# Second mixer's projection: each group's C tile moved to its sixth place, z tiles behind it

## The reference, cut to what matters

```python
proj = h @ in_w                                   # D_MODEL 1024 -> z 2048, xbc 3072, dt 64
z = proj[..., :SSD_D_INNER]
xbc = silu(_dwconv(proj[..., SSD_D_INNER:SSD_D_INNER + SSD_XBC], conv_w, conv_b))   # 5 taps
...
xh = xbc[..., :SSD_D_INNER]                       # 16 tiles of 128 columns, 4 a group
bm = xbc[..., SSD_D_INNER:SSD_D_INNER + gn]       # 4 tiles, 1 a group
cm = xbc[..., SSD_D_INNER + gn:]                  # 4 tiles, 1 a group
...
chunk_states = einsum('bcsgn,bcsgrp->bcgrpn', bm, xdt * decay_end[..., None])
def step(s, inp):
    st, dec = inp
    return s * dec[..., None, None] + st, s       # states at the chunks' starts
...
y = y * silu(z)
```

## Time and profile before

| what | before |
|---|---|
| median of 3 runs | 3686.03 us (3685.19 to 3686.39) |
| the profiled execution's own time | 3686.52 us |
| its span, first to last instruction | 3684.7 us |
| mean granted TensorE clock | 0.953 |
| TensorE busy | 3375.9 us (92%) |
| VectorE busy | 1864.7 us (51%) |
| ScalarE busy | 1276.8 us (35%) |

### The profile page before, as it was taken

The page is one execution under the profiler, slowest core; times in us unless marked ns, Lnnn a source line. Parts: engine busy times, 40 slices in busy tenths (PEclk is TensorE's granted clock), DMA queues, the critical chain, the costliest instruction groups (busy, mean ns, idle before and its releaser), DMA issues. The chain is left out here.

```text
span 3684.7 us, 58735 instructions
## 1 busy us (share of the span) xinstructions
PE 3375.9 (92%) x24055; PEld 2910.7 (79%) x24055; DVE 1864.7 (51%) x3039; ACT 1276.8 (35%) x2048; POOL 364.9 (10%) x356
## 2 busy tenths in 40 slices
PE   6999898977599999997899999789997499999998
PEld 4999674756599999996899999656664499999997
DVE  6333487765433333333545454599996533333334
ACT  4322323222133333223433233266664133332233
POOL 0000000000111111111010000000000011111111
PEclk8999898988799999998999999889998699999999
DMA  7666313254688888885243443498776488888887
GB/s 241 224 204 203 132 48 127 105 190 157 237 286 287 287 286 286 292 299 158 72 137 103 160 141 95 140 339 253 256 254 234 150 287 290 299 291 286 287 287 263
DMA packets 414015, 798.95 MB, mean 217 GB/s; under 512 B 21991, under 2 KB 108844, under 8 KB 412555
## 3 DMA queue, kind: packets, MB, share of 16 engines
q1 hardware_dynamic: 384940, 700.50, 54.1%
q0 software_dynamic: 28720, 96.31, 8.9%
q10 hardware_dynamic: 208, 0.10, 0.0%
HBM read 687.94 MB, written 108.90 MB: 216 GB/s over the span
## 5 line engine op out<-in xcount | busy, mean ns | idle before, releaser
L2441 PEld LDWEIGHTS moe_banks<-moe_xt,mix_ring 128*128 128x128 f32 x8192 | 1011.1, 191 | 5.7 <-issue 3.2
L2441 PE MATMUL moe_banks<-moe_xt,mix_ring 128*128 128x144 f32 x8192 | 1012.4, 287 | 3.1 <-ACT moe_xt L2485 3.1
L63 PE MATMUL ssd_banks<-h_leading,ssd_w_split 128*128 128x384 f32 x1920 | 416.8, 345 | 1.5 <-DVE ssd_w_split L3208 1.5
L2614 DVE TENSOR_TENSOR moe_hid<-moe_banks,moe_sg 128x128 f32<-128x128 f32 x256 | 74.7, 292 | 579.6 <-ACT moe_sg L2537 579.6
L2466 PE MATMUL moe_banks<-moe_down_parts,moe_hid_parts 128*128 128x512 f32 x1536 | 357.8, 392 | 0.0
L63 PEld LDWEIGHTS ssd_banks<-h_leading,ssd_w_split 128*128 128x128 f32 x1920 | 338.7, 189 | 16.1 <-issue 13.6
L2466 PEld LDWEIGHTS moe_banks<-moe_down_parts,moe_hid_parts 128*128 128x128 f32 x1536 | 285.8, 188 | 71.4 <-issue 13.2
L2557 DVE TENSOR_TENSOR moe_down_parts<-mix_ring,moe_down_parts 128x2048 fp32r<-128x2048 f32 x128 | 292.4, 2284 | 0.0
L3489 PE MATMUL scan_banks<-scan_w,scan_yc 128*128 128x512 f32 x576 | 253.1, 592 | 0.0
L2401 POOL DMA_INDIRECT x_dram<-moe_yc,mix_idx_quarter x128 | 166.2, 1298 | 824.8 <-DVE moe_yc L2625 795.5
L63 PE MATMUL hyin_early_banks<-h_leading,hyin_early_w_split 128*128 128x384 f32 x1152 | 244.6, 339 | 1.0 <-PEq L101 0.9
(11 more groups left out here) (472 smaller groups left out, 4375.4 us busy)
## 6 DMA issues: line engine op xcount, KB each, us to landing
mix_ring<-in_moe_w_gate SPq DMA_DIRECT2D x64, 2048.0 KB, 8.0
mix_ring<-in_moe_w_up SPq DMA_DIRECT2D x64, 2048.0 KB, 12.8
mix_ring<-in_moe_w_down SPq DMA_DIRECT2D x64, 2048.0 KB
early_ring<-in_ada_w SPq DMA_DIRECT2D x84, 512.0 KB, 6.5
scan_cum<-row_dram SPq DMA_DIRECT2D x36, 1024.0 KB, 6.2
ssd_w<-in_ssd_in_w SPq DMA_DIRECT2D x40, 512.0 KB, 4.1
s_dram<-ssdin_work SPq DMA_DIRECT2D x64, 256.0 KB, 3.5
scan_states<-s_dram SPq DMA_DIRECT2D x32, 512.0 KB, 7.8
```

Source lines behind the costliest of these rows:

```text
L63: ins = pe.matmul(out(piece), w_at(w[a], k), h_k(h[b], k, piece), start=(k == 0 and a == 0 and b == 0), stop=(k == KD - 1 and a == 1))
L2441: ins = pe.matmul(pb[:, 2 * (f % 2) + j, 0:SLOTS], ring[:, 2 * half + j, k, col:col + P], xt[:, k, :], start=(k == 0), stop=(k == KD - 1))
L2614: dve.tensor_tensor(hid[:, f % 2, :], up[:, 0:CAP_LAT], sg[:, f % 2, 0:CAP_LAT], ALU.mult).then_inc(s_hid, 1)
```

## The change

The C tile of group g moves to place j = 5 of its own group, and z tiles take j = 6, 7, 8 of all four groups; the last tile, q = 39, becomes a z tile. On VectorE, `taps` of the tile at j = 5 stand behind `rest`, `decay` and `weigh`; in all other places `taps` still stand ahead of `rest`. The lists of the other engines keep their form and follow `xbc_tile_of`: at j = 5 ScalarE now runs `xbc_tile(q)`, `end(q)`, `lead(q + 2)`, `silu(q)`, `middle(q + 1)` in all groups. The number of tiles, matmuls, taps and stores is unchanged.

```diff
     g, j = place(q)
     if g == GROUPS:
-        return Z_TILES + 2 * GROUPS - 1
+        return None
     if j == 0:
         return Z_TILES + g
     if j <= 4:
         return 4 * g + j - 1
-    if g == GROUPS - 1 and j >= 6:
-        return Z_TILES + GROUPS + j - 6
+    if j == 5:
+        return Z_TILES + GROUPS + g
     return None
 
 
 def z_tile_of(q):
-    return q if q < LEAD_IN else LEAD_IN + 4 * place(q)[0] + place(q)[1] - 5
+    return sum(xbc_tile_of(p) is None for p in range(q))
...
                 for q in range(TILES_IN):
                     end(q)
-                    if xbc_tile_of(q) is not None:
-                        taps(q)
-                    rest(q + 2)
                     if q >= LEAD_IN and place(q)[1] == 5:
+
+                        rest(q + 2)
                         for d in range(2):
                             decay(place(q)[0], 0, d)
                         for d in range(2):
                             weigh(place(q)[0], 0, d)
+                        taps(q)
+                    else:
+                        if xbc_tile_of(q) is not None:
+                            taps(q)
+                        rest(q + 2)
                     middle(q + 1)
```

## The result

| | before | after |
|---|---|---|
| median | 3686.2 us (3685.2 to 3687.6, 4 runs) | 3716.3 us (3714.7 to 3718.1, 4 runs) |
| ratio to before | | 1.0081, interval 1.0069 to 1.0092 |
| span of the profiled execution | 3684.7 us | 3712.9 us |
| mean granted clock | 0.953 | 0.951 |

The change costs 30.1 us; 32.2 had been forecast.

A forecast was written before the change was run, and what follows sets the result against it. TensorE was taken to bound the stage; 31.3 us of waits plus 9.2 us of low clock minus 8.3 us at the end gave +32.2 us, 3718.2 us on the median. The range was 3709 to 3726 us.

The forecast's parts named there:

- The bound: TensorE bounds the stage without a break, so lightening VectorE by moving C tiles gives nothing inside the groups.
- The bank and the silu: Sixth tile: TensorE's second contribution waits 7.82 us for unit 16's bank, copied behind the tap-bound silu; 31.3 us over four groups.
- The early part, the wait for weighted rows: Sixth tile: TensorE's first contribution waits 0.8 us for late weighted rows, contained in the long wait.
- the step of 1.52 us: Sixth tile: ScalarE's row copies, both weights, decays and weighted rows all move back by 1.52 us.
- No second wait behind it: After the long wait, later additions, weighted rows, weights and stores hold up nothing: 0 us.
- The clock: TensorE's idling drops its clock to half speed after each group's wait: 2.3 us a restart, 9.2 us in all.
- The end: Stage's end: a last z tile lets the next stage start earlier, gaining 8.3 us (bounds 6 to 9.1).
- Clock at full speed: Rival: the clock does not fall after the groups' waits; +23.0 us, 3709.0 us, chance 0.08.
- The faster case: Rival: unit 16 leaves its bank in time, leaving 0.8 us a group; -5.1 us, 3680.9 us, chance 0.03.
- No gain at the end: Rival: another store or the barrier holds the next stage as long as before; +40.5 us, 3726.5 us, chance 0.06.
- The lower end of the sum: Lower end of the forecast's terms: 29.6 for the waits + 6.8 for the clock - 9.1 at the end = 27.3 us.

The follow-up runs named there:

- experiment 8: Changed kernel with ScalarE's unit 16 copy ahead of the C tile's silu, and VectorE's trailing weights behind decays and weighted rows: 3677.3 us, ratio 0.9977.
- experiment 4: Changed kernel plus 36 unread matmuls on TensorE between the first and second contribution of each group's first step: 3706.8 us, ratio 1.0064.
- Experiment 1: Changed kernel with ScalarE's copy of unit 16 put ahead of the C tile's silu at the sixth place: 3681.4 us, ratio 0.9988.
- experiment 5: Changed kernel with two of the four tap passes of each C tile cut to 64 columns instead of 1154: 3709.7 us, ratio 1.0061.
- experiment 6: Changed kernel with the last group's sixth place a z tile again and the last C tile back at place 39: 3712.9 us, ratio 1.0075.
- experiment 2: Kernel before, with its last C tile moved to the third group's ninth place so that a z tile is last: 3677.9 us, ratio 0.9981.
- experiment 3: Changed kernel with VectorE's taps again ahead of trailing weights, decays and weighted rows at the sixth place: 3707.6 us, ratio 1.0061.

## Why the prediction was right

*The bound.* Right. TensorE is the limit throughout, and the lighter load of VectorE in the last group gave nothing: with one C tile in every group and no waits (experiment 8) a group takes 132.25 us, as it did before, and from the last group's first contribution to its last tile it is 56.06 us in both, with 31.75 us of work for VectorE instead of 43.80.

*The bank and the silu.* Right in place, releaser and size. Forecast 7.82 us at the second pair of loads, measured 7.78; 31.3 us for the four groups, measured 4 x 7.55 = 30.2 in the groups' length (experiment 4). Experiment 1 takes it away, experiment 5 shortens it in step with the taps. The early part, the wait for weighted rows, had been put at 0.8 us and is 0.95 at the loads. The weighted rows start 6.94 us after ScalarE's first instruction instead of 5.44, so the step of 1.52 us was right; experiment 8 shows that the wait goes when the trailing weights stand behind the weighted rows.

*No second wait behind it.* Right: TensorE has no other wait in the stage.

*The clock.* The mechanism was right: it fell in all four groups. The size was 2.3 us a group, 9.2 in all; measured were 2.0 and 8.2 (38.4 - 30.2). Half of the 3.4, 5.3, 2.8 and 5.0 us at the lower level after the restarts sums to 8.3. That the sizes came so close is in part luck. The prediction took 4.9 us from the restart at 1807.13, but TensorE had started again at 1803.62 already, and the clock was at 0.50 there too (1802.00:1812.00 in the earlier trace rows); from that restart it was low for 8.4 us, 1.54 us of idling among them. And the four stretches here differ by up to a factor of two.

The Trainium skill, "TensorE: Matmul & The Clock Gate" (HAM oscillation), prices throttled time at 1 - 1.2/2.4, which is this half, and the trace agrees: 8.3 against 8.2 us. Part 1 of the same page of the Trainium skill puts the ramp at under 1% of a typical span, and 8.2 us are indeed 0.2% of this one. But they are 8 of the change's 30 us, and experiment 4 gives them back, so here they could not be left out.

*The end.* 8.3 us forecast, 7.8 measured. The z store came as forecast. What holds the stage now is the stores of the context states. SyncE's waits from 2404 on in the changed kernel show it: SyncE waits 2.7 us for the states to land (L2912), and then only 0.2 us for the other engines (L2849). Before, it had waited 8.4 us for them.

```profile
SPq L2912 <- DMA out_new_state<-ssdin_ctx_state: 2.7, 1, 2.7
...
SPq L2849 <- PEq L2849: 0.2, 1, 0.2
```

and before:

```profile
SPq L2849 <- PEq L2849: 8.4, 1, 8.4
...
SPq L2912 <- DMA out_new_state<-ssdin_ctx_state: 1.7, 1, 1.7
```

The z store is issued at 2406.64 and lands 5.2 us later, at 2411.8; the last state store is issued at 2410.07 and lands 3.4 us later, at 2413.5. Two terms of the prediction were off and partly cancel, and that is luck. The last state store was to land 6.5 us after the last projection (2375.4 - 2368.92) and lands after 8.3. The barrier was to take 2.6 us and takes 1.5, up to the load at 2415.01. The first is late because the four issues take 3.83 us instead of 2.90 (the third alone 1.55 instead of some 0.6) and their time to landing is 3.9 us instead of 2.4 (medians). ScalarE's second state copy, which now waits 0.17 us for TensorE, is not the reason: it is done at 2407.59, and the third issue starts at 2408.16. In experiment 6, where a C tile is last again, the issues take 2.91 us and land in 2.4. That it is the z store beside them which slows them fits this, but no run separates the two.

*The rivals and the range.* Clock at full speed, 3709.0: experiment 4 is that case, 3706.8. The faster case, 3680.9: experiment 1 is it, 3681.4. No gain at the end: refuted by the 9.81 us and by experiment 2. The lower end of the sum, 27.3, has 6.8 us for the clock, which no step of the prediction gives (its own lower bound was 0); 8.2 was measured.

*The order on VectorE,* which the prediction took as given, is a loss by itself as the change has it: with the taps ahead (experiment 3) it is 8.7 us less. Putting weighted rows first serves the wait that costs 0.95 us and lengthens the one that costs 7.8, since the taps release the silu, and the silu stands in front of the bank's copy.

## What to carry to other kernels

When a longer job is put in a slot of an in-order engine, look at what stands behind it on that engine, and who waits for that: here a copy of 0.26 us behind a silu held the bound engine for 7.8 us, because the silu waited for the taps, and because with two side banks a unit needs the one before last emptied. Put copies that free shared buffers ahead of anything that waits. And price an idle time of several us of a bound TensorE with the half-speed stretch that follows it; that was a fifth of the groups' loss here (8.2 of 38.4 us).

## What the runs showed of the hardware

The cost of the clock's fall is not one number. Idle times of 4.2 to 6.5 us were followed by 2.8 to 6.0 us at 1.2 GHz (worked out from the mean clock of 7 us, as above), and the same 6.46 us, within one execution, by 2.8 to 5.3 us, so 1.4 to 3.0 us were lost each time; the shorter waits of experiments 3 and 5 had the longer stretches on the mean (5.1 and 5.5 us against 4.1). The spread is not noise between executions alone: the three restarts of experiment 6 read 0.76, 0.63 and 0.80, like the first three of the changed kernel (0.76, 0.62, 0.80). So the mean of one kernel's four restarts could not be taken for that of another. The idle times of 0.68 us alone, in experiment 1, were followed by no fall: the clock there reads 1.00 in each of the four stretches of 130 us from 1850 to 2370.
